# Modulation products of vectors 4 to 7 moved from TensorE to GpSimd

## The reference, cut to what matters

```python
mod = jax.nn.silu(c) @ w_mod[l] + b_mod[l]            # (1, 1024) @ (1024, 6144)
sh_m, sc_m, gt_m, sh_f, sc_f, gt_f = [m[:, None, :] for m in jnp.split(mod, N_MOD, axis=-1)]
h = rms_norm(x, g_mix_norm[l]) * (1.0 + sc_m) + sh_m
proj = h @ w_in[l]
(q_a, k_a, v_a, q_i, k_i, w_i, q_b, k_b, v_b, gate_a, gate_b) = jnp.split(proj, split_at, axis=-1)
# ... two attentions with norms and rotations of q and k, an index that picks keys ...
x = x + gt_m * (merged @ w_out[l])
h = rms_norm(x, g_ffn_norm[l]) * (1.0 + sc_f) + sh_f
```

## Time and profile before

| | us |
|---|---|
| median of 3 runs (lowest, highest) | 1494.52 (1492.64, 1495.31) |
| the profiled execution's own time | 1488.22 |
| its span, first to last instruction | 1486.2 |
| PE busy | 1439.9 (97% of the span) |
| DVE busy | 848.0 (57%) |
| ACT busy | 689.8 (46%) |
| POOL busy | 36.2 (2%) |
| POOL's two stretches of work between 40 and 130 us | 73.9 to 76.7 and 92.1 to 94.1 |

### The profile page before, as it was taken

The page is one execution under the profiler, slowest core; times in us unless marked ns, Lnnn a source line. Parts: engine busy times, 40 slices in busy tenths (PEclk is TensorE's granted clock), DMA queues, the critical chain, the costliest instruction groups (busy, mean ns, idle before and its releaser), DMA issues.

```text
span 1486.2 us, 17970 instructions
## 1 busy us (share of the span) xinstructions
PE 1439.9 (97%) x6904; PEld 1153.0 (78%) x6904; DVE 848.0 (57%) x1032; ACT 689.8 (46%) x881; POOL 36.2 (2%) x53
## 2 busy tenths in 40 slices
PE   6999999999999999999999999999999998999998
PEld 3757777688888888888888888788888865788887
DVE  2686865654556445466764454476454758645544
ACT  2554463544344434454454344654344567553442
POOL 0010100000000000000000000110000020000000
PEclk9999999999999999999999999999999999999999
DMA  9853666455554655546555555555555510455551
GB/s 346 297 199 124 245 214 243 156 195 187 180 198 152 215 175 193 185 157 198 194 174 197 175 193 179 167 169 189 187 191 191 184 57 30 142 185 183 195 188 69
DMA packets 188165, 271.14 MB, mean 182 GB/s; under 512 B 8381, under 2 KB 134149, under 8 KB 188101
## 3 DMA queue, kind: packets, MB, share of 16 engines
q1 hardware_dynamic: 186448, 267.01, 53.5%
q10 hardware_dynamic: 1492, 2.98, 0.5%
q0 software_dynamic: 160, 0.26, 0.2%
HBM read 269.19 MB, written 1.05 MB: 182 GB/s over the span
## 4 chain that ended last, share of the span: by engine, by line
PE 86%; DVE 5%; DMA 3%; ACT 3%; issue 2%; SPq 1%; POOL 0%; DVEq 0%; ACTq 0%
PE bank L1801 26%; PE bank L1803 26%; PE bank L1802 26%; PE bank L1831 2%; DVE w_lo_ring L1311 2%; ACT w_hi_ring L966 1%; PE bank L1971 1%; DMA raw_ring<-in_w_in_dram 1%; DMA arena<-in_w_mod_dram 1%; PE bank L1939 1%; DMA raw_ring<-in_w_gate_up_dram 1%; PE bank L2025 1%; PE bank L2124 1%; DVE arena L1671 0%; PE bank L2103 0%
## 5 line engine op out<-in xcount | busy, mean ns | idle before, releaser
L1311 DVE TENSOR_TENSOR w_lo_ring<-raw_ring,w_hi_ring 128x2048 fp32r<-128x2048 f32 (+1 forms) x226 | 513.8, 2277 | 408.2 <-ACT w_hi_ring L1254 329.4
L1801 PE MATMUL bank<-w_hi_ring,h_hi 128*128 128x512 f32 x1360 | 543.3, 400 | 2.8 <-DVE h_lo L1455 1.0
L1803 PE MATMUL bank<-w_hi_ring,h_lo 128*128 128x512 f32 x1360 | 531.4, 391 | 0.0
L1802 PE MATMUL bank<-w_lo_ring,h_hi 128*128 128x512 f32 x1360 | 530.6, 390 | 0.0
L1254 ACT ACTIVATE w_hi_ring<-raw_ring 128x2048 fp32r<-128x2048 f32 x158 | 302.6, 1915 | 295.5 <-PE bank L1803 292.2
L1801 PEld LDWEIGHTS bank<-w_hi_ring,h_hi 128*128 128x128 f32 x1360 | 256.0, 188 | 67.8 <-issue 15.3
L1803 PEld LDWEIGHTS bank<-w_hi_ring,h_lo 128*128 128x128 f32 x1360 | 255.7, 188 | 55.0
L1802 PEld LDWEIGHTS bank<-w_lo_ring,h_hi 128*128 128x128 f32 x1360 | 256.2, 188 | 49.3
L1801 PE MATMUL bank<-w_hi_ring,f_hi 128*128 128x512 f32 (+1 forms) x456 | 177.0, 388 | 0.0
L1803 PE MATMUL bank<-w_hi_ring,f_lo 128*128 128x512 f32 (+1 forms) x456 | 175.9, 386 | 0.0
L1802 PE MATMUL bank<-w_lo_ring,f_hi 128*128 128x512 f32 (+1 forms) x456 | 175.7, 385 | 0.0
(11 more groups left out here) (258 smaller groups left out, 855.1 us busy)
## 6 DMA issues: line engine op xcount, KB each, us to landing
raw_ring<-in_ffn_w_gate_up_dram SPq DMA_DIRECT2D x176, 512.0 KB
raw_ring<-in_ffn_w_down_dram SPq DMA_DIRECT2D x44, 1024.0 KB
raw_ring<-in_w_in_dram SPq DMA_DIRECT2D x22, 1024.0 KB
raw_ring<-in_w_gate_up_dram SPq DMA_DIRECT2D x44, 512.0 KB
arena<-in_w_mod_dram SPq DMA_DIRECT2D x18, 1024.0 KB, 7.2
raw_ring<-in_w_down_dram SPq DMA_DIRECT2D x11, 1024.0 KB
raw_ring<-in_conv_w_in_dram SPq DMA_DIRECT2D x16, 512.0 KB
raw_ring<-in_w_mod_dram SPq DMA_DIRECT2D x6, 1024.0 KB
```

Of the source, the lines that this page charges most:

```text
L1311: dve.tensor_tensor(w_lo[:, u % RING, 0:words], raw[:, r % RING, 0:words], w_hi[:, u % RING, 0:words].bitcast(F32), ALU.subtract).then_inc ...
L1801: pe.matmul(dst, hi, whi, start=start, stop=False)
L1802: pe.matmul(dst, hi, wlo, start=False, stop=False)
L1803: return pe.matmul(dst, lo, whi, start=False, stop=stop)
```

## The change

Vector 7 joins vectors 4 to 6 in the side buffers. For these four the eight `mrow` items are gone, and with them ACT's copies and DVE's additions. In their place stand items `pmod`, which POOL works through: it multiplies the four 128 x 512 pieces of a half, in place, by a column each (32 times `silu(c)`), adds the four products, and leaves the sum in `acc` (first half) or adds it to `acc` (second half). Each half then counts up `pool_half`. `mod_sum` on PE now sums all 128 partitions with a matrix of 1/32. SP's reload of a side buffer waits for `pool_half`, and so does ACT before it writes the gates into the same place.

```diff
-SIDE_MODS = (4, 5, 6)
+SIDE_MODS = (4, 5, 6, 7)
...
-    t[0:P:32, C_SEL:C_SEL + P] = 1.0
+    t[:, C_SEL:C_SEL + P] = 1.0 / 32
...
+    def mod_pool(m, half):
+        return [dict(kind="pmod", m=m, half=half)]
...
-    part("ki", 0, 0, 1, [mod_row(4, 0), evac("ki"), mod(4, 1)])
-    part("qb", 0, 0, 2, [mod_row(4, 1), [dict(kind="kir")], mod(5, 0)], [[dict(kind="tp", stage="kiu", g=0)], []])
-    part("qb", 0, 1, 2, [mod_sum(4), tgroup("qi", 2), tgroup("ki", 1), mod_row(5, 0), evac("qb"), mod(5, 1)])
-    part("kb", 0, 0, 2, [mod_row(5, 1), mod(6, 0)])
-    part("kb", 0, 1, 2, [mod_sum(5), tgroup("qb", 2), mod_row(6, 0), evac("kb"), mod(6, 1)], [index[0], [], index[1], index[2]])
+    part("ki", 0, 0, 1, [evac("ki"), mod_pool(4, 0), mod(4, 1)])
+    part("qb", 0, 0, 2, [mod_pool(4, 1), [dict(kind="kir")], mod(5, 0)], [[dict(kind="tp", stage="kiu", g=0)], []])
+    part("qb", 0, 1, 2, [mod_sum(4), tgroup("qi", 2), tgroup("ki", 1), evac("qb"), mod_pool(5, 0), mod(5, 1)])
+    part("kb", 0, 0, 2, [mod_pool(5, 1), mod(6, 0)])
+    part("kb", 0, 1, 2, [mod_sum(5), tgroup("qb", 2), evac("kb"), mod_pool(6, 0), mod(6, 1)], [index[0], [], index[1], index[2]])
...
-    part("vb", 0, 0, 2, [mod_row(6, 1)], [[], index[3], index[4], index[5] + rot[0]])
-    part("vb", 0, 1, 2, [mod_sum(6), evac("vb")], [rot[1], index[6], index[7], rot[2]])
+    part("vb", 0, 0, 2, [mod_pool(6, 1), mod(7, 0)], [[], index[3], index[4], index[5] + rot[0]])
+    part("vb", 0, 1, 2, [mod_sum(6), evac("vb"), mod_pool(7, 0), mod(7, 1)], [rot[1], index[6], index[7], rot[2]])
...
-    part("ga", 0, 0, 2, [topk(0, 0)], [tgroup("kb", 2) + inside[0][0]] + inside[0][1:])
+    part("ga", 0, 0, 2, [topk(0, 0), mod_pool(7, 1)], [tgroup("kb", 2) + inside[0][0]] + inside[0][1:])
...
-    part("ga", 1, 1, 2, [evac("ga", 1), topk(0, 3), mod(7, 0)], inside[3])
-    part("qa", 0, 0, 2, [mod_row(7, 0), mod(7, 1), topk(1, 0)])
-    part("qa", 0, 1, 2, [mod_row(7, 1), evac("qa"), mod(8, 0)])
+    part("ga", 1, 1, 2, [evac("ga", 1), topk(0, 3)], inside[3])
+    part("qa", 0, 0, 2, [topk(1, 0)])
+    part("qa", 0, 1, 2, [evac("qa"), mod(8, 0)])
...
-    freed = {r: ("raw_done", e[1] + 1) if e[0] == "unit" else ("t_done", find["tg", "mrow", (e[2], e[1])] + 1)
+    freed = {r: ("raw_done", e[1] + 1) if e[0] == "unit" else ("pool_half", find["pool", e[1], e[2]])
+             if e[1] in SIDE_MODS else ("t_done", find["tg", "mrow", (e[2], e[1])] + 1)
...
+                if k == "pmod":
+                    side = -1 - find["raw", item["m"], item["half"]]
+                    if item["done"] == 0:
+                        pool.wait_ge(sem("c_ready"), 1)
+                        tick.step(pool.tensor_scalar(c_32, c_act[:, :, 0], 32.0, None, ALU.mult))
+                    if item["half"] == 0:
+                        pool.wait_ge(sem("t_done"), find["sum of", item["of"] - 2] + 1)
+                    pool.wait_ge(sem(f"side_full{side % SIDE}"), 16 * (side // SIDE + 1))
+                    a = acc[:, item["of"] % 2, :]
+                    w = early[2 + side % SIDE]
+                    for kk in range(4):
+                        c = 4 * item["half"] + kk
+                        ins = pool.tensor_scalar(w[:, kk, :], w[:, kk, :], c_32[:, c:c + 1], None, ALU.mult)
+                        tick(ins)
+                    tick.wait()
+                    tick(pool.tensor_tensor(w[:, 0, :], w[:, 0, :], w[:, 1, :], ALU.add))
+                    tick.step(pool.tensor_tensor(w[:, 2, :], w[:, 2, :], w[:, 3, :], ALU.add))
+                    if item["half"] == 0:
+                        ins = pool.tensor_tensor(a, w[:, 0, :], w[:, 2, :], ALU.add)
+                    else:
+                        tick.step(pool.tensor_tensor(a, a, w[:, 0, :], ALU.add))
+                        ins = pool.tensor_tensor(a, a, w[:, 2, :], ALU.add)
+                    ins.then_inc(sem("pool_half"), 1)
...
                     elif st in ("ga", "gb"):
+                        act.wait_ge(sem("pool_half"), 2 * len(SIDE_MODS))
...
                     elif st == "mod":
-                        wait_group(pe, find["tg", "mrow2", g] if g in LATE_MODS else find["tg", "mrow", (1, g)])
+                        if g in SIDE_MODS:
+                            pe.wait_ge(sem("pool_half"), find["pool", g, 1])
+                        else:
+                            wait_group(pe, find["tg", "mrow2", g] if g in LATE_MODS else find["tg", "mrow", (1, g)])
```

More of the change, by code:

```diff
@@ L474, in make_plan @@
                 last_p = item["tg"], count.get("it tp", 0)
+        if k == "pmod":
+            item["of"], item["done"] = number("mrow") // 2, number("pmod")
         if k == "ffn":
@@ L496, in make_plan @@
             find["of", item["g"]] = item["of"]
+        if k == "pmod":
+            find["of", item["m"]] = item["of"]
+            find["pool", item["m"], item["half"]] = item["done"] + 1
         if k == "tp" and st == "mod":
@@ L668, in two_block_program @@
         wi = carve(TT, IH)
+        c_32 = carve(KT)
         rl = carve(2, T)
@@ L1880, in _ @@
                             pe.wait_ge(sem("small_full"), 16 * 4)
-                            pe.matmul(b[0][0:60, 0:256], sel[0:1, 0:60], b1r[0:1, c, :], start=True, stop=False)
+                            pe.matmul(b[0][0:60, 0:256], const[0:1, C_COSH:C_COSH + 60], b1r[0:1, c, :], start=True, stop=False)
                         for kk in range(8):
```

## The result

The changed kernel takes 1540.18 us (median of 4 runs, 1535.9 to 1541.39) beside 1493.58 us for the kernel before (one run more than in the table above): a ratio of 1.0317, 95% interval 1.0299 to 1.0336, or +46.6 us. The forecast was slower, 1515 us with a range up to 1529. So the direction was right, the size was not: +20 was forecast, and the time lies above the range. Of the rivals, the shared port (1530) came nearest, and still 10 us short.

The account below looks back on a forecast made before the run. Whatever frees the side buffers was taken to stand in the weights' path, so POOL's halves delay units: 20.2 - 2.4 + 2 = +20 us on the profiled 1488.22, or 1508; with 6.3 us to the runs' median, 1515 us, range 1502 to 1529.

Parts of the forecast that it names:

- the shared port: Rival, chance 0.14: POOL and DVE shut each other out, halves take 12 and 13 us, +36 us, 1530 us.
- the price of a half: POOL's half priced from memset rows (0.57 and 0.99 us) plus waits for DVE: 7 us first, 8 us second.
- The bound of 12 us: Upper end for a half on POOL: each instruction waits for a DVE one, some of these of 2.29 us.
- -2.4 + 2: Terms after the stalls: vector 7's two products gone, -2.4 us; clock loss behind two restarts, +2 us.
- The bounds beside the chances: The main forecast's 1508 to 1523 us for halves of 5.5 to 9 us, given chance 0.66.
- qb's copy: On ACT, following ki's copy with no product's copy between: starts at 67.8 instead of 70.38, 2.6 us early.
- The chain of roots and loads: POOL's roots precede halves, halves free buffers for SP's side loads, units queue behind: unit 8 11.2 us late, unit 10's subtraction 20.2.
- Second stall: Unit 10 waits behind kb's root and vector 6's first half: on ACT at 119.1, subtraction on DVE 20.2 us late.
- ga's copy: ACT's write of the gates, waiting for POOL's last half: that half ends at 134, copy near 145, no cost.
- The gain of 9.8 us: On PE, eight removed products at 1.2 us each: 9.8 us at most.
- the faster rival: Rival, chance 0.06: waits on POOL are hidden and the eight products gained, -9.8 us, 1485 us.
- The clock: PE's granted clock sinks to the lower level behind long stands: 2 us for two restarts, between 0 and 4.

Follow-up runs that it names:

- e2: The changed kernel with side loads for vectors 5 to 7 later in SP's list, behind ring loads, and sums of vectors 4 to 6 later on PE: 1526.71 us.
- e11: The changed kernel with each half's arithmetic replaced by memsets, 9 and 11 a half (5.2 and 6.4 us), all waits kept: 1505.86 us, ratio 1.0083.
- e3: The changed kernel with the halves' multiplications left out, all but 8 columns of one; additions remain: 1516.98 us, ratio 1.0168.
- e9: The changed kernel with each half's arithmetic replaced by memsets, halves of 9.9 and 11.1 us, all waits kept: 1521.64 us, ratio 1.0193.
- e10: The changed kernel with each half's arithmetic replaced by 22 and 24 memsets (12.8 and 14.0 us), all waits kept: 1534.95 us, ratio 1.0283.
- e1: The changed kernel with the first halves of vectors 5 and 6 ahead of qb's and kb's roots in POOL's list: 1521.89 us, ratio 1.0199.
- e8: The kernel before with the eight products of vectors 4 to 7 cut to one matmul of 8 columns each, all else left: 1489.03 us, ratio 0.9981.
- e4: The kernel before with seven halves' worth of arithmetic added on POOL in unused columns, nobody waiting for it: 1500.03 us, ratio 1.0059.
- e7: The kernel before with 154 memsets of 128x512 added on POOL, nobody waiting for them: 1492.23 us, ratio 1.0005.
- e6: The changed kernel with roots behind the halves, each multiplication written as a two-operand product with a repeated column: 1528.19 us, ratio 1.0250.

## Why the prediction was wrong

**The step that failed first is the price of a half:** "I price a multiplication (one operand) like the first and an addition (two operands) like the second ... I take 7 us for a first half and 8 for a second." They took 12.5 and 14.2. POOL's own part is 10.1 and 11.4 (e2's last two halves, 135.70 to 157.21, with DVE idle): a multiplication costs 1.545 us, not 0.57, and an addition 1.26, not 1.0. A memset only writes; every kind of 128x512 arithmetic measured here took longer, and I read its price as an estimate. The bound of 12 us that I had written beside it was near the truth, but for another reason (waits for DVE), and I chose by the nearest row. DVE's rows add 2.4 and 2.8 us a half.

**The price alone does not give the time.** In the prediction's steps each microsecond more in a first half makes unit 10's subtraction two microseconds later. With the 12.07 and 11.43 us of the two halves that stand in that path it would be 29.7 us late, and the time 1494.5 + 29.7 - 2.4 + 2 = 1524 us, still inside the range. The subtraction was 43.0 us late (143.84 against 100.84). (The bounds beside the chances, 1508 to 1523 for halves of 5.5 to 9 us, are wider than the steps, which give 1511 to 1518.)

**The second step that failed is qb's copy, "2.6 us early".** It was 9.1 us late, and qb's root ended at 85.8 instead of 74.0. PE came to vector 4's sum at 67.9 (65.3 before; 62.7 by the shared-port rival's own working), after the 2.88 us wait for a DVE subtraction at 60.54, and then waited there 7.01 us for POOL. The shared-port rival held that second wait, the forecast did not: its halves of 7 and 8 us end before PE arrives. Other runs show the two apart:

| vector 4's halves, us | DVE's two-operand rows grow | PE waits at vector 4's sum | qb's root ends | unit 8 on ACT |
|---|---|---|---|---|
| 7, 8 (forecast) | not counted | 0 | 74.0 | 89.1 |
| 5.2, 6.4 (e11) | no | 0 | 73.6 | 86.5 |
| 6.0, 7.2 (e3) | yes | 0 | 79.6 | 94.6 |
| 9.9, 11.1 (e9) | no | 2.66 | 76.2 | 93.9 |
| 12.8, 14.0 (e10) | no | 8.68 | 82.2 | 102.8 |
| 12.65, 17.0 (the change) | yes | 7.01 | 85.8 | 105.8 |

The wait of e10:

```profile
71.14 2.04 PE L1982 MATMUL bank<-arena,const 128*128 128x512 f32 x2 [8.68 <-POOL arena L932]
```

**The chain of roots and loads was right for short halves.** In e11, with 5.2 us, the prediction's steps put unit 8 on ACT at 87.3 and unit 10 at 115.5; they came at 86.54 and 115.28. For long halves it lacked the wait at vector 4's sum, and so a microsecond of half costs 3.4 us from e11 to e9 and 4.6 from e9 to e10, not 2. By these runs the change's +46.6 comes apart as +12.7 at the bare price of a memset (e11), +15.8 up to POOL's own rate (e9), +13.3 for the 2.9 us that DVE's work adds to a half (e10), and +4.8 between memsets and arithmetic of the same length; that last part's intervals (up to 1.0309, from 1.0299) touch, so its size is not settled. So some 28 us are POOL's own, and some 18 come from POOL and DVE meeting.

**Second stall, 43.0 us in place of 20.2.** The same chain again: unit 8 and kb's sums are late, kb's root starts at 120.65, and the half behind it ends at 134.04. Between unit 8 and kb's root the forecast had 1.2 us won; there was nothing won (27.95 and 28.5 us late).

**ga's copy.** "that new wait costs nothing; if halves took 12 us it would begin to count": they did, and it does: 2.37 us at the end of POOL's last half. From kb's root on POOL works through four halves in a row, 122.59 to 174.26, so the copy could not come earlier whatever the loads did (first and last row):

```profile
122.59 7.55 POOL L931 TENSOR_SCALAR arena<-arena 128x512 f32<-128x512 f32 x4
...
172.98 1.28 POOL L940 TENSOR_TENSOR arena<-arena 128x512 f32<-128x512 f32 x1
```

That is where e2 stops, with a wait of 25.41 us at 157. In e1 the copy starts 0.55 us behind POOL's end, but ACT's row before it waited for DVE, so POOL is not shown to hold it there. From unit 10 on the forecast's -2.4 + 2 would leave 42.6 us, and the profiled execution is 47.7 slower; beside the 2.37 us the rest of that is not taken apart.

**The gain of 9.8 us was not there.** A row of PE's timeline gave the products' price, but not what ran behind them (the earlier trace rows shows 1.39 us of PE's wait for DVE): e8 gives back 2.6 us of 9.6, and as far as its trace shows, longer waits for DVE and a lower granted clock behind them took most of the rest. The forecast's sum used 2.4 us of it, so that error moved it by little; of the faster rival's 9.8 us, PE's products alone would have brought 2.6.

**The clock.** The low clock behind the stands is there (0.50 from 100 to 110 us). From 122.59 on POOL's list sets ga's copy, so what PE lost to the clock between then and 174.3 is not in the sum; what it lost before, on the way to the two roots, is, and no run shows how much. So the 2 us are not confirmed. e8 shows that such a loss can be larger: about 4.7 us behind two stands of 2.6 and 2.2 us.

**The rule.** The Trainium skill (SBUF — State Buffer, Who interferes with whom) has DVE and GpSimd exclude each other where DVE reads two operands from SBUF and GpSimd reads SBUF, but not where GpSimd only writes. The trace agrees with that in both directions: POOL's 1.26 us additions took 3.2 us beside a DVE subtraction, DVE's 485 ns rows took 883 beside POOL's arithmetic (e4) and stayed at 485 beside memsets (e7, ratio 1.0005). In this form it does not cover the one-operand copy, which grew beside memsets (196 to 410 ns). I gave the rival 0.14 because the stalls leave DVE idle, which is true of the halves at 97.95 and 134.02 (13.4 us still, with one addition of 3.21) and not of vector 4's second half (17.0).

## What to carry to other kernels

Price work on an engine by rows of the same kind of instruction, and where there are none, build the case on the upper bound: an instruction that only writes says little of one that reads. Before counting a removed instruction as a gain, ask which engine used its time, and look at the granted clock behind the new waits; leaving the instruction out in the kernel before is a cheap test. Put a corrected price back into the prediction's own sum: if it still does not give the time, a second step failed. And where an in-order engine gets long work, look for every short item behind it: here two roots of 3 us, placed ahead of or behind a half, moved 18 us.

## What the runs showed of the hardware

- On POOL the multiplication of 128x512 by a column (one operand in SBUF and a scale for each partition) took 1.545 us, more than the addition of two operands (1.26) and the product with a repeated column (1.0). The Trainium skill (GPSIMD Engine Reference, Engine selection) calls one-input work on GpSimd roughly line-rate; the trace does not agree for this multiplication, which is slower than the two-operand addition, and the measurement decides here.
- Some 90 us of POOL's memsets (0.58 us for 512 columns) ran beside DVE at no cost that can be told in the kernel's time, and DVE's two-operand rows kept their length; a one-operand copy inside SBUF grew from 196 to 410 ns (e7). Some 92 us of arithmetic cost the kernel 6.6 us (e4).
- DVE rows of 0.18 us took 1.29 and 1.07 beside POOL's products of 1.0 us (e6), so short instructions lose most beside long ones.
- Around and behind PE's waits of 2.57 and 2.25 us in e8 the granted clock was 0.70 from 70 to 80 us and 0.83 from 110 to 120; in the kernel before, with waits of 0.64 and 1.39 us there, it was 1.00 in both.
